# A decoder layer on one core: GpSimd's low part of the third operand in four pieces, spread behind four weights

## The reference, cut to what matters

```
a = RMSNorm(x);  u = a @ w_in            # "in":  12 pairs of column blocks, and the gates
h = mLSTM(q, k, v, gates), y = short convolution
x = x + concat(h, y) @ w_out             # "out": 4 pairs
f = RMSNorm(x)
x = x + (silu(f @ w_gate) * (f @ w_up)) @ w_down   # "ffn": 11 + 11 pairs, and down
x = x + sigmoid(x @ w_pg) * RMSNorm(p @ w_ple)     # "pg": 4 pairs
```

## Time and profile before

| what | value |
|---|---|
| runs | 2565.9, 2566.76, 2578.99 us; median 2566.76 us |
| the profiled execution | 2566.95 us, its span 2565.2 us |
| mean granted clock of TensorE | 0.994 of full |
| TensorE busy | 2463.4 us, 96% of the span, 15829 matmuls |
| GpSimd busy | 1120.3 us, 44%, 1125 instructions |
| VectorE, ScalarE busy | 1448.4 us (56%), 905.7 us (35%) |
| transfers | 501.04 MB, 195 GB/s |

### The profile page before, as it was taken

How to read it: one execution, slowest core, us unless ns; L and a number is a source line. 1 busy time by engine, 2 the same in 40 slices (tenths; PEclk the granted TensorE clock), 3 DMA queues, 4 the chain that set the end, 5 groups by cost and what they waited for, 6 DMA issues and landing times.

```text
span 2565.2 us, 41412 instructions
## 1 busy us (share of the span) xinstructions
PE 2463.4 (96%) x15829; PEld 2397.8 (93%) x15829; DVE 1448.4 (56%) x2305; ACT 905.7 (35%) x1688; POOL 1120.3 (44%) x1125
## 2 busy tenths in 40 slices
PE   8999889999999999999999999999999999999998
PEld 7898889999999998999999999998899999999997
DVE  7668887555545674477633333568357763332355
ACT  5344453334334542434212111354134522221233
POOL 6767876778776531223222222343212322222233
PEclk9999999999999999999999999999999999999999
DMA  7656645567655756585545644575657564565444
GB/s 224 220 203 243 211 164 205 192 227 282 214 202 189 230 190 192 165 285 170 189 129 189 210 162 144 172 226 190 193 188 261 163 201 148 199 212 176 170 132 150
DMA packets 285047, 501.04 MB, mean 195 GB/s; under 512 B 18427, under 2 KB 182612, under 8 KB 284342
## 3 DMA queue, kind: packets, MB, share of 16 engines
q1 hardware_dynamic: 212182, 273.59, 31.6%
q10 hardware_dynamic: 72672, 224.82, 26.3%
HBM read 374.70 MB, written 123.65 MB: 194 GB/s over the span
## 4 chain that ended last, share of the span: by engine, by line
PE 73%; DVE 6%; DMA 5%; POOL 2%; issue 2%; ACT 1%; DVEq 0%; ACTq 0%; POOLq 0%; SPq 0%
PE bank L609 23%; PE bank L611 22%; PE bank L610 22%; DMA wring<-weight_parts 3%; POOL wring L2712 2%; DMA weight_parts<-wring 1%; DVE qlo L1804 1%; DMA xs<-x_prompt 1%; PE bank L733 1%; PE bank L744 1%; PE bank L799 0%; PE bank L809 0%; DVE ess L2431 0%; PE bank L722 0%; PE bank L752 0%
## 5 line engine op out<-in xcount | busy, mean ns | idle before, releaser
L2712 POOL TENSOR_TENSOR wring<-wraw,wring 128x256 fp32r<-128x256 f32 (+1 forms) x782 | 859.2, 1118 | 1138.3 <-ACT wring L1301 1136.0
L609 PE MATMUL bank<-qhi,wring 128*128 128x352 f32 (+1 forms) x3588 | 1168.2, 326 | 57.5 <-POOL wring L2712 14.7
L611 PE MATMUL bank<-qhi,wring 128*128 128x352 f32 (+1 forms) x3588 | 1151.4, 321 | 0.0
L610 PE MATMUL bank<-qlo,wring 128*128 128x352 f32 (+1 forms) x3588 | 1149.2, 320 | 0.0
L609 PEld LDWEIGHTS bank<-qhi,wring 128*128 128x128 f32 x3588 | 678.1, 189 | 86.2 <-issue 59.2
L610 PEld LDWEIGHTS bank<-qlo,wring 128*128 128x128 f32 x3588 | 678.2, 189 | 0.0
L611 PEld LDWEIGHTS bank<-qhi,wring 128*128 128x128 f32 x3588 | 676.0, 188 | 0.0
L1301 ACT ACTIVATE wring<-wraw 128x512 fp32r<-128x512 f32 x531 | 331.5, 628 | 708.4 <-PE bank L611 552.0
L609 PE MATMUL bank<-hid,wring 128*128 128x352 f32 (+1 forms) x1056 | 339.7, 322 | 11.3 <-DVE wide L2514 7.1
L611 PE MATMUL bank<-hid,wring 128*128 128x352 f32 (+1 forms) x1056 | 338.4, 320 | 0.0
L610 PE MATMUL bank<-hid,wring 128*128 128x352 f32 (+1 forms) x1056 | 337.6, 320 | 0.0
(11 more groups left out here) (316 smaller groups left out, 2309.5 us busy)
## 6 DMA issues: line engine op xcount, KB each, us to landing
wring<-weight_parts ACTq DMA_DIRECT2D x418, 512.0 KB, 4.5
weight_parts<-wring SPq DMA_DIRECT2D x201, 512.0 KB, 4.7
wraw<-w_down SPq DMA_DIRECT2D x33, 1024.0 KB, 7.1
wraw<-w_in SPq DMA_DIRECT2D x14, 1024.0 KB, 7.8
wraw<-w_gate SPq DMA_DIRECT2D x11, 1024.0 KB, 6.4
wraw<-w_up SPq DMA_DIRECT2D x11, 1024.0 KB, 6.4
wraw<-w_in SPq DMA_DIRECT2D x44, 256.0 KB, 5.0
wraw<-w_gate SPq DMA_DIRECT2D x44, 256.0 KB, 3.7
```

Of the source, the lines that this page charges most:

```text
L609: nc.tensor.matmul(o, hi, mh, start=begins, stop=False, skip_group_check=True)
L610: nc.tensor.matmul(o, hi, ml, start=False, stop=False, skip_group_check=True)
L611: return nc.tensor.matmul(o, lo, mh, start=False, stop=ends, skip_group_check=True)
L2712: last = nc.gpsimd.tensor_tensor(low_[:, ks, :], w.src[:, ks, :], high_[:, ks, :], ALU.subtract)
```

## The change

`low_of` on GpSimd takes a list of k tiles and issues one operation for each of them, of N elements in place of 4N. The waits stand before k tile 0, the increment of low2 on the operation of k tile 3. In "out" the four come behind the `ahead()` calls j = 8 to 11, in "pg" behind the steps s = 2 to 5, in "ffn" behind j = 9, 10 and 11 (the last with two), and in "in" all at once as before.

```diff
@@ -2718,12 +2718,16 @@
                 if n_lo[0] < len(entries) and entries[n_lo[0]].spare is not None:
                     one_ahead()
 
-            def low_of(q, st):
-
-                pool.wait_ge(high, HIGH[(q.n, st, 2)])
-                if st == "ffn":
-                    pool.wait_ge(src_ready, SOURCE[(q.n, "ffn", 5)])
-                nc.gpsimd.tensor_tensor(qlo[:, 2, :, 0:q.N], source(q, st, 2), qhi[:, 2, :, 0:q.N], ALU.subtract).then_inc(low2, 1)
+            def low_of(q, st, ks):
+
+                if 0 in ks:
+                    pool.wait_ge(high, HIGH[(q.n, st, 2)])
+                    if st == "ffn":
+                        pool.wait_ge(src_ready, SOURCE[(q.n, "ffn", 5)])
+                for k in ks:
+                    last = nc.gpsimd.tensor_tensor(qlo[:, 2, k, 0:q.N], source(q, st, 2)[:, k, :], qhi[:, 2, k, 0:q.N], ALU.subtract)
+                if 3 in ks:
+                    last.then_inc(low2, 1)
 
             def roots_of_x(q, half):
                 pool.wait_ge(x_sq, NTILE * q.n + (3, 6)[half])
@@ -2818,8 +2822,8 @@
 
             def pg_after(q):
                 def after(s):
-                    if s == 2:
-                        low_of(q, "pg")
+                    if 2 <= s <= 5:
+                        low_of(q, "pg", (s - 2,))
                     if q.n < 2 and s in (8, 13):
                         roots_of_x(supers[q.n + 1], s // 13)
                 return after
@@ -2832,7 +2836,7 @@
             ahead()
             for q in supers:
                 if q.n:
-                    low_of(q, "in")
+                    low_of(q, "in", range(4))
                 plain_pair(q, in_after(q))
                 ahead()
                 ahead()
@@ -2840,8 +2844,8 @@
                     pair(in_after(q), 7 * i)
                 for j in range(14):
                     ahead()
-                    if j == 8:
-                        low_of(q, "out")
+                    if 8 <= j <= 11:
+                        low_of(q, "out", (j - 8,))
                 for i in range(2, 4):
                     pair(nothing, 0)
                 for k in range(4):
@@ -2852,8 +2856,8 @@
                     if p == 0:
                         for j in range(14):
                             ahead()
-                            if j == 9:
-                                low_of(q, "ffn")
+                            if j in (9, 10, 11):
+                                low_of(q, "ffn", ((0,), (1,), (2, 3))[j - 9])
                         continue
                     pair(nothing, 0)
                     if down_before(p) is not None:
```

## The result

The changed kernel took 2579.84 us, median of 20 runs, beside 2572.44 for the kernel before (20 runs too). The ratio is 1.0024, 95% interval 1.0015 to 1.0033: +6.2 us (3.9 to 8.5). The forecast was +7.3 us on an execution of 2566.95. In absolute terms 2574 stands against 2579.84, some 6 us short, and nearly all of that is the starting point: the execution that was counted from was a quick one (see the last experiment). The profiled execution of the changed kernel took 2578.8 us.

A forecast was written before the change was run, and what follows sets the result against it. TensorE, busy 96% of the span, was taken as the bound, so only its idling counts. "out" +4.1, "ffn" +3.5, "pg" +2.4 and "in" -2.7 sum to +7.3 us: 2574 us, range 2565.5 to 2580.

The forecast's parts named there:

- A piece: Every low-part stage: one of the four GpSimd operations takes 0.85 us, between 0.80 and 0.92.
- "out": Super 0: fourth piece, queued behind weight 15 (w15), delays product 12 (p12, in P3) by 3.4 us; net +4.1.
- "ffn": Super 0: fourth piece ends at 373.7, product 12 (p12) starts 3.8 us later than before; net +3.5.
- the sixth that I had booked there: "ffn", super 0: the 2.92 us wait for VectorE at 394.15 gives back a sixth of itself.
- "pg": First pair's P3 (p6) starts later by 0.75, 0.4 and 1.3 us in supers 0, 1, 2; sum +2.4.
- "in": Supers 1 and 2: VectorE gets a turn between pieces; -2.15 before, +0.8 at P3, -2.7 us for both.
- The rival without turns for VectorE: At "in" each next piece starts first, so the -2.7 goes: 2577 us, chance 0.17.
- The clock: Super 0, "out" and "ffn": after the long idle the low clock adds 1.7 us each (0 to 1.7).
- The base: Whole kernel before the change: profiled execution 2566.95 us, median of the runs 2566.76, the forecast's starting point.
- The slower rival: "out", "ffn": VectorE's sums no earlier, clock falls after both idle stretches; +15.1 us, 2582, chance 0.08.
- p12 of "ffn" after 375: Product 12 of "ffn" starting after 375 us would decide for the slower rival; forecast start 373.8.
- The hidden-cost rival: "out", "ffn": late low part hidden in TensorE's waits for VectorE, these two net about +0.5; 2567, chance 0.15.

The follow-up runs named there:

- the last experiment: The kernel before and the changed kernel, both unchanged, profiled once more on one chip: 2576.4 us and 2580.51 us (ratio 1.0017).
- the first pair of traces: First profiles of the kernel before (2566.95 us, the one the prediction rested on) and of the changed kernel (2578.8 us).
- the second pair: Second profiles of the kernel before and of the changed kernel, both unchanged, on one chip: 2576.4 and 2580.51 us.
- the first trace: Profile of the kernel before, nothing changed, on which the prediction rests: 2566.95 us.

## Why the prediction was right

The sum, +7.3 against +6.2 (3.9 to 8.5), came out with its mechanisms mostly right: the fourth piece is late by what the queue puts in front, and VectorE gets its turn at "in". Its closeness is partly luck, for several terms were off, some against each other.

- **A piece:** 0.85 us taken, 0.94 measured, just over the upper bound of 0.92.
- **"out":** forecast idle 3.4 us, measured 4.48 and 4.45. The fourth piece ended at 286.3, forecast 286.0. TensorE came 0.8 us sooner. The way to 286.3 was another than argued. The prediction let w15 wait for ScalarE's high part from 283.29 on and granted 0.6 us for its coming earlier; it was there by 282.3, and GpSimd never stood still. Against that the pieces (0.92 to 1.23 us, 0.85 forecast) and the weights (1.89 to 2.13, 1.8 forecast) were each a little longer, and the two errors nearly cancel. The net shift by the end of the stage was 4.1 forecast and about 4.3 in the trace; the wait of 1.07 us at 300.21 did vanish. A run with this part alone gives +2.1 (-1.3 to 5.1) by its times and 4.3 by its trace.
- **"ffn":** the working was right within 0.2 us where it followed the queue: the fourth piece forecast at 373.7, which with the stage's own 4.1 us of delay is 377.8, measured 377.6. The earlier high part came as argued (sum 1.07 us). Idle was 6.26 and 4.89, forecast 5.0. Net +3.5 forecast, +4.7 in the first pair of traces (8.8 at 427 less 4.1 at 326), +3.5 in the second pair; of the two waits for VectorE the 1.49 went, as said, and the 2.92 was still 3.01, so the sixth that I had booked there wasn't given back. Alone +5.7 (1.5 to 9.8).
- **"pg":** +0.75, +0.4 and +1.3 forecast; the waits grew by 0.95, 0.79 and 1.65 (a piece takes 0.90 to 1.10 here, not 0.85). The times say +0.5 (-2.3 to 3.3).
- **"in":** -2.7 forecast, -5.1 (-8.2 to -2.1) measured alone. In the traces TensorE gains 2.25 and 1.8 us where the waits were and gives 0.6 and 0.3 back in the products behind, where 0.8 each was booked: I had the last piece end 0.7 us after P3's turn, and it ended 0.17 us after. That is -3.2 for both supers, close to the forecast. What the prediction lacked is the low clock. It took from the first trace that nothing follows a wait of 2.37 us; in the second trace of the same kernel ten slow matmuls do:

```profile
908.69 0.63 PE L609 MATMUL bank<-qhi,wring 128*128 128x352 f32 x1 [2.39 <-DVE sg L1831]
909.12 0.49 PE L610 MATMUL bank<-qlo,wring 128*128 128x352 f32 x1
```

The seven traces with one operation at "in" have 14 such waits, of 2.25 to 2.39 us, and behind 8 of them stand 9 to 11 slow matmuls; at the ten starts of "in" with pieces there are none. By these counts that is another 1.5 us of gain, an estimate (8/14 of two stretches, ten matmuls each, 0.13 us). The rival without turns for VectorE is refuted: four pieces take 8.36 us because VectorE runs between them.

- **The clock:** +1.7 us each for "out" and "ffn", taken from one product at 1.2 GHz behind 4.15 us of idle time. That the low clock follows such a wait is borne out. Behind all four waits of 3.8 to 4.5 us before P3 of "out" come 10 or 11 slow matmuls, behind all four of 4.9 to 6.3 us before P3 of "ffn" 12 to 19; the other eight traces have none right behind P3 of "out", not even the one that waits 2.61 us there. The size over the stage is smaller than booked, because the other traces have slow stretches nearby at waits that all twelve have. From 340 to 415 us of the first trace, and over the same work in the others, the four traces with the spread in "ffn" have 39 slow matmuls in the mean (35 to 43), the other eight 27 (18 to 36): +1.6 us. From 266 to 310 it is 23 (21 to 26) against 17 (11 to 26) for the spread in "out": +0.7. So some 2.3 us stand where 3.4 were booked. This compares traces of ten kernels and no run changed the clock alone, so it is an estimate; without any such term the sum is 3.9, the lower end of the interval of the measured difference. When the low clock falls in front of a wait for a semaphore it is hidden in it, as in the run with "out" alone.
- **The base:** 2566.95 us was taken as the time of the kernel before, with a median of three beside it; over 20 to 35 runs the median is 2572 to 2576. One of the three times, 2578.99, lay 12 us above the other two and could have told it.

The slower rival had priced w15's high part as not earlier; it was earlier, and the difference didn't pass 0.5%. Its sign, p12 of "ffn" after 375, did come true, at 377.74, but only because the mark left out the 4.1 us that the stage itself is late; with "ffn" alone p12 starts at 374.24. The hidden-cost rival (2567) falls by the waits and by the +9.5 us of the three spreads together, though the times of "out" and of "pg" alone can't exclude it for these parts.

By the rule of the Trainium skill (SBUF — State Buffer, "SBUF: two separate sides") an instruction keeps the port pair for its whole length; the traces agree: 4.20 us became 1.94 when the GpSimd instruction in front was cut in four. The dispatch that the Trainium skill (GPSIMD Engine Reference, "2.1 Instruction dispatch") charges to each instruction is there but small: four pieces of 0.94 us against 3.22 for one operation is 3.76 less 3.22 over three, 0.18 us for each piece more.

## What to carry to other kernels

In an in-order queue that waits for its own consumers, spreading a piece of work over the queue delays its last part by everything put in front; cut an operation only to let another engine in between, and keep the pieces together unless their reader is later than the last of them. The turns of the other engine make the cut piece of work longer (3.19 became 4.84 us in "ffn", 4.47 became 8.36 at "in"), so it pays only where that engine is the one that is awaited. Here four short operations in one place, where VectorE stood waiting, gave 5 us, and the operations that were spread over three other stages cost 9.5. And before adding up microseconds against one trace, look whether that execution is an ordinary one: count its stretches at the low clock.

## What the runs showed of the hardware that wasn't expected

GpSimd and VectorE, both with work queued on operands in SBUF, take turns: four GpSimd operations of 352 elements took 2.2 us each beside VectorE and 0.94 alone, while VectorE's additions with a PSUM operand kept their 0.51 us. The twelve traces have 92 stretches at the low clock after 240 us, 8 to 19 matmuls long, and every one begins within 3.3 us of the end of an idle stretch of TensorE of 1.7 to 6.3 us. Which of the shorter waits is followed by one changes from one execution of the same kernel to the next; all 21 waits of 3.6 us or more are followed. The 61 more slow matmuls in one of two traces of the kernel before answer to 8 of the 9.4 us between their spans. So a wait that is taken away can be worth more than its length, and one trace doesn't tell how much.
